# A decoder trunk on one core: the first norm made from the banks in which x is turned, and two weight splits moved in the attention

## The chip, the core and the metric

The kernel runs on one core of a Trainium2 chip. Five engines work side by side, each through its own list of instructions, and meet only at semaphores: TensorE (matrix products, called PE in the profile), VectorE (DVE), ScalarE (ACT), GpSimd (POOL) and SyncE (SP), which here only starts DMAs. The metric is the device time of one execution in microseconds, as a median over runs.

## The reference

Two layers over x of 256 tokens by 1024 columns, all in float32. Each layer adds half a SwiGLU feed-forward (2816 wide), a token mixer, and half a second feed-forward, each behind an RMS norm; a final norm ends it.

```
x = x + 0.5 * swiglu(rmsnorm(x, g1), w_gate, w_up, w_down)
h = rmsnorm(x, g_mix)
x = x + (hybrid_gdn_shortconv(h, ...) if layer == 0 else sliding_window_attention(h, ...))
x = x + 0.5 * swiglu(rmsnorm(x, g2), ...)

rmsnorm(x, g) = x * rsqrt(mean(x * x) + 1e-6) * g
swiglu(x)     = (silu(x @ w_gate) * (x @ w_up)) @ w_down
attention: 16 query heads, 4 key and value groups, window 128, rotary, a sink per head;
           p = exp(s - mx) / (sum(exp(s - mx)) + exp(sink - mx));  o = p @ v;  o @ w_o + b_o
```

## The kernel before

**Products.** Every float32 matrix is split in two parts that TensorE takes at full rate: a high part (a rounded copy) and a low part (the difference). A product is three matmuls: high by high (L349), low activation by high weight (L350), high activation by low weight (L354).

**Weights.** All weights stream through a ring of three slots in chunks of 1 MB (128 x 2048), numbered over the whole program. For each, SyncE loads `raw` (`load`, L302; it waits until the low half of the chunk three before is made), ScalarE makes `w_hi` (`split_hi`, L310; it waits until TensorE has used the chunk three before), VectorE makes `w_lo` (`split_lo`, L324; `split_lo_half`, L330, does it in two instructions). TensorE uses the chunk in `column_chunk` (L357, 48 matmuls of 256 columns), `down_chunk` (L624) or, in the attention, `token_chunk` (L1419) and `out` (L1544).

**Layout of x.** x is kept transposed in `xT`, as four pairs of 128-row tiles. At the start x is loaded in two column halves (L1807, L1808), TensorE turns it pair by pair into the four banks ACC (L1976), VectorE copies each bank to `xT` (L444), ScalarE makes the high half of h = x times the norm's weight (L419) and VectorE its low half (L431). The squares for the norm (L407), their sum (`norm_sum`, L459, VectorE, three additions), the sum over rows on TensorE (`norm_ss`, L392), the reciprocal (`norm_var`, L469) and the root (`norm_rstd`, L477) go beside the first matmuls, since the norm's factor is applied to the results of the projections. The first feed-forward takes chunk 0 (gate) and 1 (up), then `norm_ss`, chunk 2 (gate of the next group), chunk 3 (its up) and chunk 4 (the first down chunk); TensorE waits for `var_ready`, which the reciprocal raises, before chunk 3, since that chunk goes to the bank in which the sum stood. The first down chunk waits for `act_ready`, the low half of the gated activation (L582). ACC is free for the down products only when x is out of it.

**Order.** Each engine's order is written out by hand in the blocks at the end (L1801 to L1987). In the first stage ScalarE makes all high halves of h, the high half of chunk 0 in two pieces (L317), four squares, loads the table of the root, makes the high halves of chunks 1 and 2, starts the loads of the constants (`load_rest`, L1773: 832 KB and four small ones, on ScalarE's DMA queue), and goes on with chunks 3 and 4.

**Attention.** `swa_tensor` (L1415) takes six projection chunks c to c+5, and between and behind them, for four groups of heads, the scores (L1477), the turning of the probabilities (L1496), the values (L1510), the turning of the outputs (L1523) and the output projection, whose chunks 0 to 3 are c+6 to c+9. `soft` (L1684, VectorE) masks the scores and finds the maxima, `exps` (L1608, ScalarE) makes the exponentials; the turned probabilities of a group leave three banks, two by ScalarE (L1623) and one by VectorE (L1715), and the scores of the group two later wait for these copies. On VectorE the low half of chunk c+7 (output chunk 1) stands at the end of step m=4 and that of c+8 (output chunk 2) at the end of m=5, ahead of the copy of group 1.

## Time and profile before

| | us |
|---|---|
| median of 3 runs (lowest to highest) | 1023.87 (1023.36 to 1026.7) |
| the profiled execution's own time | 1026.56 |
| its span, first to last instruction | 1024.8 |
| TensorE busy (share of the span) | 996.1 (97%) |
| VectorE busy | 623.9 (61%) |
| ScalarE busy | 474.7 (46%) |
| GpSimd busy | 70.6 (7%) |
| mean granted TensorE clock | 0.995 |

Busy times are of one profiled execution; the span leaves out the short stretches around the first and the last instruction. A line of a timeline gives the start, the duration, the engine, the source line, what is written and read, how many of the same stand in the row, and in brackets how long the engine was idle before and what ended that idle time. Matmuls overlap, so the start of one is before the end of the last.

### The profile page before, as it was taken

Reading aid. Unit: us, or ns where it says so; the run is one execution under the profiler, and the core shown is the slowest. Engines: PE = TensorE matmul, PEld = TensorE weight load, DVE = VectorE, ACT = ScalarE, POOL = GpSimd, SP = SyncE. Lnnn points to the kernel's source line nnn. Section 1 sums busy time; section 2 is a strip of 40 time slices with the busy share of each in tenths; the row PEclk is TensorE's granted clock in tenths of the full one; section 3 lists DMA queues with packets and bytes.
Section 4 is the critical chain, followed back from the end, with each engine's and each line's share of the span. In section 5 each row is a group of like instructions: output and inputs, shape, how many; then the busy total and the mean of one; then the engine's idle time right before and its main releaser. Section 6 shows DMA issues by size and latency. Waiting matters only on the chain.

```text
span 1024.8 us, 19751 instructions
## 1 busy us (share of the span) xinstructions
PE 996.1 (97%) x8302; PEld 976.0 (95%) x8302; DVE 623.9 (61%) x651; ACT 474.7 (46%) x521; POOL 70.6 (7%) x63
## 2 busy tenths in 40 slices
PE   6999999999999999999999999999998999999997
PEld 6999999988999999999999999999997999999996
DVE  5755555788764376555548655555788376555553
ACT  5543444645553265443446543443656264443442
POOL 0110010100000001010110101010100001100100
PEclk9999999999999999999999999999999999999999
DMA  7666565454422246656665665656443045566651
GB/s 245 219 210 195 197 204 183 146 152 136 124 86 80 83 164 207 205 173 198 199 196 170 212 196 174 205 174 231 158 165 110 15 139 190 190 193 192 203 184 42
DMA packets 136035, 172.80 MB, mean 169 GB/s; under 512 B 4293, under 2 KB 123322, under 8 KB 135994
## 3 DMA queue, kind: packets, MB, share of 16 engines
q1 hardware_dynamic: 134176, 171.26, 51.7%
q10 hardware_dynamic: 1818, 0.96, 0.3%
q8 instruction: 31, 0.51, 0.2%
q14 instruction: 10, 0.08, 0.0%
HBM read 171.15 MB, written 1.05 MB: 168 GB/s over the span
## 4 chain that ended last, share of the span: by engine, by line
PE 87%; DVE 7%; ACT 3%; DMA 1%; issue 1%; POOL 0%; DVEq 0%; POOLq 0%; SPq 0%; ACTq 0%
PE bank L349 24%; PE bank L350 24%; PE bank L354 24%; PE bank L638 6%; DVE w_lo L327 2%; PE bank L1429 2%; ACT w_hi L315 1%; DMA raw<-in_ffn_w_up 1%; PE bank L873 1%; PE bank L857 1%; PE bank L868 1%; DMA work<-in_x 1%; DVE work L1272 1%; ACT h_hi_rest L419 0%; PE bank L1489 0%
## 5 line engine op out<-in xcount | busy, mean ns | idle before, releaser
L327 DVE TENSOR_TENSOR w_lo<-raw,w_hi 128x2048 fp32r<-128x2048 f32 x154 | 354.4, 2301 | 190.0 <-ACT w_hi L315 190.0
L349 PE MATMUL bank<-h_hi_rest,w_hi 128*128 128x256 f32 x1428 | 394.8, 278 | 0.4 <-DVE h_lo_rest L431 0.4
L350 PE MATMUL bank<-h_lo_rest,w_hi 128*128 128x256 f32 x1428 | 393.7, 277 | 0.0
L354 PE MATMUL bank<-h_hi_rest,w_lo 128*128 128x256 f32 x1428 | 385.2, 277 | 0.0
L315 ACT ACTIVATE w_hi<-raw 128x2048 fp32r<-128x2048 f32 x159 | 302.7, 1909 | 155.7 <-PE bank L354 139.7
L349 PEld LDWEIGHTS bank<-h_hi_rest,w_hi 128*128 128x128 f32 x1428 | 269.2, 188 | 0.8 <-DVE h_lo_rest L431 0.6
L350 PEld LDWEIGHTS bank<-h_lo_rest,w_hi 128*128 128x128 f32 x1428 | 269.1, 188 | 0.0
L354 PEld LDWEIGHTS bank<-h_hi_rest,w_lo 128*128 128x128 f32 x1428 | 264.1, 188 | 0.0
L349 PE MATMUL bank<-act_hi,w_hi 128*128 128x256 f32 x480 | 132.7, 276 | 1.1 <-DVE act_lo L582 1.1
L354 PE MATMUL bank<-act_hi,w_lo 128*128 128x256 f32 x480 | 132.6, 276 | 0.0
L350 PE MATMUL bank<-act_lo,w_hi 128*128 128x256 f32 x480 | 132.6, 276 | 0.0
L615 POOL TENSOR_TENSOR silu_r<-silu,work 128x512 f32<-128x512 f32 x44 | 60.5, 1375 | 785.9 <-ACT silu L528 785.9
L528 ACT ACTIVATE silu<-gate 128x512 f32<-128x512 f32 x44 | 27.8, 631 | 145.5 <-DVE gate L570 145.5
L349 PEld LDWEIGHTS bank<-act_hi,w_hi 128*128 128x128 f32 x480 | 90.1, 188 | 1.3 <-issue 1.3
L350 PEld LDWEIGHTS bank<-act_lo,w_hi 128*128 128x128 f32 x480 | 90.2, 188 | 0.0
L354 PEld LDWEIGHTS bank<-act_hi,w_lo 128*128 128x128 f32 x480 | 90.1, 188 | 0.0
L538 ACT ACTIVATE act_hi<-act 128x512 fp32r<-128x512 f32 x40 | 25.3, 633 | 132.0 <-PE bank L354 86.1
L349 PE MATMUL bank<-h_hi_first,w_hi 128*128 128x256 f32 x204 | 60.8, 299 | 7.0 <-DVE w_lo L341 3.5
L582 DVE TENSOR_TENSOR act_lo<-act,act_hi 128x512 fp32r<-128x512 f32 x40 | 27.7, 692 | 62.7 <-ACT act_hi L538 62.7
L354 PE MATMUL bank<-h_hi_first,w_lo 128*128 128x256 f32 x204 | 57.1, 280 | 0.0
L350 PE MATMUL bank<-h_lo_first,w_hi 128*128 128x256 f32 x204 | 56.4, 277 | 0.0
L349 PE MATMUL bank<-m_hi,w_hi 128*128 128x256 f32 (+1 forms) x200 | 55.8, 286 | 0.0
(276 smaller groups left out, 1258.1 us busy)
## 6 DMA issues: line engine op xcount, KB each, us to landing
raw<-in_ffn_w_up SPq DMA_DIRECT2D x44, 1024.0 KB, 5.3
raw<-in_ffn_w_down SPq DMA_DIRECT2D x44, 1024.0 KB, 4.8
raw<-in_ffn_w_gate SPq DMA_DIRECT2D x43, 1024.0 KB, 5.4
raw<-in_hyb_w_in SPq DMA_DIRECT2D x14, 1024.0 KB, 5.3
raw<-in_swa_w_qkv SPq DMA_DIRECT2D x6, 1024.0 KB, 5.0
raw<-in_hyb_w_out SPq DMA_DIRECT2D x4, 1024.0 KB, 5.6
raw<-in_swa_w_o SPq DMA_DIRECT2D x4, 1024.0 KB, 5.2
work<-in_x SPq DMA_DIRECT2D x2, 512.0 KB, 5.8
```

Source lines behind the costliest of these rows:

```text
L315: nc.scalar.activation(w_hi[slot(ch)][:], raw[:, slot(ch), :], ACT.Copy).then_inc(hi_split, 1)
L327: nc.vector.tensor_tensor(w_lo[slot(ch)][:], raw[:, slot(ch), :], w_hi[slot(ch)][:].bitcast(F32), ALU.subtract).then_inc(lo_split, 1)
L349: nc.tensor.matmul(out_ap, w_hi[s][:, wcols], mv_hi, start=start, stop=False, skip_group_check=True)
L350: i = nc.tensor.matmul(out_ap, w_hi[s][:, wcols], mv_lo, start=False, stop=False, skip_group_check=True)
L354: return nc.tensor.matmul(out_ap, w_lo[s][:, wcols], mv_hi, start=False, stop=stop, skip_group_check=True)
L528: nc.scalar.activation(silu[:], gate[:], ACT.Silu).then_inc(silu_ready, 1)
L538: nc.scalar.activation(hi.rearrange("p a b -> p (a b)"), act[:], ACT.Copy) \
L582: nc.vector.tensor_tensor(lo.rearrange("p a b -> p (a b)"), act[:], hi.rearrange("p a b -> p (a b)").bitcast(F32), ALU.subtract).then_inc( ...
L615: nc.gpsimd.tensor_tensor(silu_r[:].rearrange("p (a s) -> p a s", a=2), silu[:].rearrange("p (a s) -> p a s", a=2), over_rows(rstd_half[:] ...
L638: last = nc.tensor.matmul(o, st[:, k, tok], mv[s][:, cols], start=False, stop=False, skip_group_check=True)
L857: i = mm(head((AUX, AUX2)[b], h), one(step_m[n % 2], b, h), one(inv, b, h), start=True, stop=True)
L1429: i = mm(bk[:, b * CW:(b + 1) * CW], st[kt][:, b * P:(b + 1) * P], mv[s][:, kt * CW:(kt + 1) * CW], start=(start and n_pass == 0), stop=(s ...
```

## The change

x is loaded in three parts: two quarters of the columns on SyncE's queue and the half behind them on ScalarE's, between the loads of the norms' weights. In the first norm ScalarE and VectorE read x straight from the banks in which it was turned, and VectorE's four copies to `xT` are replaced by four of ScalarE (`keep_x`), one ahead of chunk 3's high half and three behind it. The high half of chunk 1 stands ahead of the squares, that of chunk 2 behind them and ahead of the table. The low half of chunk 0 is made in two pieces (`first_lo`) between the products of h, and TensorE takes the low products of a stage's first chunk in two halves of the rows. VectorE sums the squares ahead of chunk 2's low half, which is made in two pieces, and makes chunk 3's low half behind the reciprocal. In all four feed-forwards TensorE waits for `var_step` (the addition ahead of the reciprocal) in place of `var_ready`. The loads of the constants go to SyncE's queue, behind the first group's. TensorE multiplies a matrix of ones eight times ahead of the turning of x (`warm`). In the attention the low halves of output chunks 1 and 2 are moved on VectorE to ahead of and behind the last group's softmax.

```diff
+        def first_lo(dve, half):
+            dve.wait_ge((first_half_split, hi_split)[half], 1)
+            cols = slice(half * 1024, (half + 1) * 1024)
+            nc.vector.tensor_tensor(w_lo[0][:, cols], raw[:, 0, cols], w_hi[0][:, cols].bitcast(F32),
+                                    ALU.subtract).then_inc((first_lo_half, lo_split)[half], 1)
...
-              .then_inc((lo_half_split, lo_split)[part], 1)
+              .then_inc((half_done or lo_half_split, lo_split)[part], 1)
...
-                pe.wait_ge(lo_split, number(ch) + 1)
-                for ft in range(HG):
-                    for kt in range(KT):
-                        last = step(kt, ft, False, kt == KT - 1, 1)
+                for half in range(2):
+                    if first_chunk and half == 0:
+                        pe.wait_ge(first_lo_half, 1)
+                    else:
+                        pe.wait_ge(lo_split, number(ch) + 1)
+                    for ft in range(HG):
+                        for kt in range(half * KT // 2, (half + 1) * KT // 2):
+                            last = step(kt, ft, False, kt == KT - 1, 1)
             else:
                 for ft in range(HG):
                     if early is not None and ft == 0:
-                        pe.wait_ge(lo_half_split, early)
+                        pe.wait_ge(*early)
...
+        def turned(j):
+            return ACC[j][:]
+        def first_norm_scalar(act_e):
+            for j in range(PAIRS):
+                act_e.wait_ge(acc_done, j + 1)
+                for kt in (2 * j, 2 * j + 1):
+                    g = norm_column(0) + kt
+                    i = nc.scalar.activation(h_hi[kt], ACC[j][:, (kt % 2) * SEQ:(kt % 2 + 1) * SEQ], ACT.Copy,
+                                             scale=vecT[:, g:g + 1])
+                i.then_inc(h_hi_ready, 1)
+                if j % 2:
+                    first_split(act_e, j // 2)
+            split_hi(act_e, (1, 0), check=False)
+            for j in range(PAIRS):
+                act_e.wait_ge(h_ready, j + 1)
+                nc.scalar.activation(sq[:, j, :], turned(j), ACT.Square).then_inc(sq_ready, 1)
+            split_hi(act_e, (2, 0), check=False)
+            load_table(ACT.Sqrt)
+        def keep_x(act_e, j):
+            pair = xT[:, 2 * j:2 * j + 2, :].rearrange("p a b -> p (a b)")
+            nc.scalar.activation(pair, turned(j), ACT.Copy).then_inc(x_updated, 1)
+        def first_norm_vector(dve):
+            for j in range(PAIRS):
+                dve.wait_ge(h_hi_ready, j + 1)
+                for kt in (2 * j, 2 * j + 1):
+                    g = norm_column(0) + kt
+                    i = nc.vector.scalar_tensor_tensor(out=h_lo[kt],
+                                                       in0=ACC[j][:, (kt % 2) * SEQ:(kt % 2 + 1) * SEQ],
+                                                       scalar=vecT[:, g:g + 1], in1=h_hi[kt].bitcast(F32),
+                                                       op0=ALU.mult, op1=ALU.subtract)
+                i.then_inc(h_ready, 1)
+                if j % 2:
+                    first_lo(dve, j // 2)
...
                 if before_pair is not None:
                     before_pair(j)
                 act_e.wait_ge(x_updated, PAIRS * n + j + 1)
-                if n:
-                    act_e.wait_ge(sq_summed, n)
-                    act_e.wait_ge(ss_ready, n)
+                act_e.wait_ge(sq_summed, n)
+                act_e.wait_ge(ss_ready, n)
                 for kt in (2 * j, 2 * j + 1):
                     g = norm_column(n) + kt
                     i = nc.scalar.activation(h_hi[kt], xT[:, kt, :], ACT.Copy, scale=vecT[:, g:g + 1])
                 i.then_inc(h_hi_ready, 1)
-                if n:
-                    square(j)
...
-                if n == 0:
-                    nc.vector.tensor_copy(pair, banks[j][:]).then_inc(x_updated, 1)
-                elif bias is None:
+                if bias is None:
...
+        def load_rest(sp):
+            sp.dma_start(kon[:, P:K_END], t["constants"][:, P:K_END]).then_inc(rest_loaded, 16)
+            sp.dma_start(sinks[:], t["swa_sinks"][0].partition_broadcast(P)).then_inc(rest_loaded, 16)
...
+            sp.wait_ge(wba_cleared, 1)
+            sp.dma_start(wba_pad.rearrange("p (k c) -> p k c", k=KT)[:, :, 0:8],
+                            t["hyb_w_in"][0].rearrange("(k p) f -> p k f", p=P)[:, :, 4 * KEY:4 * KEY + 8]) \
...
             group(0)
+            if f == 0:
+                load_rest(sp)
             with sp.Fori(1, NG - 1) as i:
                 group(i)
...
-            column_chunk(pe, (c0 + 1, 0), UP, h_hi, h_lo, early=n + 1)
+            column_chunk(pe, (c0 + 1, 0), UP, h_hi, h_lo, early=(lo_half_split, n + 1))
...
-            column_chunk(pe, (c0 + 2, 0), AUX2, h_hi, h_lo)
-            pe.wait_ge(var_ready, n + 1)
+            column_chunk(pe, (c0 + 2, 0), AUX2, h_hi, h_lo, early=(first_lo_half, 2) if f == 0 else None)
+            pe.wait_ge(var_step, n + 1)
             column_chunk(pe, (c0 + 3, 0), AUX, h_hi, h_lo)
...
-                if m:
+                if m in (1, 2, 3):
                     split_lo(dve, (c + m + RING, 0))
             copy_probs(1)
             lo_o(0)
+            split_lo(dve, (c + 4 + RING, 0))
             soft(3)
+            split_lo(dve, (c + 5 + RING, 0))
             norm_o(1)
...
-            sp.dma_start(x_in[:, :, 0:D // 2], xt[:, :, 0:D // 2]).then_inc(x_loaded, 16)
-            sp.dma_start(x_in[:, :, D // 2:D], xt[:, :, D // 2:D]).then_inc(x_loaded2, 16)
+            sp.dma_start(x_in[:, :, 0:D // 4], xt[:, :, 0:D // 4]).then_inc(x_loaded, 16)
+            sp.dma_start(x_in[:, :, D // 4:D // 2], xt[:, :, D // 4:D // 2]).then_inc(x_loaded2, 16)
...
             for k, name in enumerate(("ffn1_norm", "mix_norm", "ffn2_norm")):
+                if k == 1:
+                    act_e.dma_start(x_in[:, :, D // 2:D], xt[:, :, D // 2:D]).then_inc(x_loaded3, 16)
...
-                    norm_scalar(act_e, n, lambda j: j >= 2 and first_split(act_e, j - 2))
-                    split_hi(act_e, (1, 0), check=False)
-                    split_hi(act_e, (2, 0), check=False)
-                    load_rest(act_e)
+                    first_norm_scalar(act_e)
+                    keep_x(act_e, 0)
                 else:
                     norm_scalar(act_e, n, (lambda j: j < 2 and split_hi(act_e, (c - 1 + j, 0))) if mixed else None)
                     if mixed:
                         split_hi(act_e, (c + 1, 0))
                     split_hi(act_e, (c + 2, 0))
                 split_hi(act_e, (c + 3, 0))
-                if kind == "swa":
+                for j in range(1, PAIRS if n == 0 else 1):
+                    keep_x(act_e, j)
+                if n == 0 or kind == "swa":
...
-                norm_vector(dve, n, banks, ready,
-                            vecT[:, V_BO:V_BO + KT] if n and stages[n - 1][0] == "swa" else None,
-                            (c - 1, 0) if mixed else None)
...
                 if n == 0:
-                    split_lo(dve, (c, 0))
+                    first_norm_vector(dve)
+                else:
+                    banks, ready = update(n)
+                    norm_vector(dve, n, banks, ready,
+                                vecT[:, V_BO:V_BO + KT] if stages[n - 1][0] == "swa" else None,
+                                (c - 1, 0) if mixed else None)
                 for part in range(2):
                     split_lo_half(dve, (c + 1, 0), part, kind == "swa")
                 if n == 0:
                     dve.wait_ge(vec_turned, 2)
                     nc.vector.tensor_copy(vecT[:, FIRST_VEC:NVEC], AUX2[:, FIRST_VEC:NVEC]).then_inc(vec_ready, 1)
-                if kind == "swa":
+                if n == 0:
+                    norm_sum(dve, n)
+                    for part in range(2):
+                        split_lo_half(dve, (c + 2, 0), part, half_done=first_lo_half)
+                elif kind == "swa":
                     norm_sum(dve, n)
...
                 norm_var(dve, n)
+                if n == 0:
+                    split_lo(dve, (c + 3, 0))
                 dve.wait_ge(rstd_ready, n + 1)
...
+            def warm(times):
+                for k in range(times):
+                    nc.tensor.matmul(AUX2[:, 0:P], ones[:], ones[:], start=True, stop=True)
+            pe.wait_ge(set_up, 1)
+            warm(4)
             pe.wait_ge(ident_loaded, 16)
             pe.wait_ge(first_vec_loaded, 16)
             nc.tensor.transpose(AUX[:, 0:FIRST_VEC], vec_rows[0:FIRST_VEC, :], ident[0:FIRST_VEC, 0:FIRST_VEC]) \
               .then_inc(vec_turned, 1)
-            pe.wait_ge(x_loaded, 16)
+            warm(4)
             for j in range(PAIRS):
-                if j == PAIRS // 2:
-                    pe.wait_ge(x_loaded2, 16)
+                if j <= PAIRS // 2:
+                    pe.wait_ge((x_loaded, x_loaded2, x_loaded3)[j], 16)
                 for kt in (2 * j, 2 * j + 1):
                     for b in range(TB):
                         o = (kt % 2) * SEQ + b * P
```

## Rows read from the trace of the kernel before

**Rows 1.** windows of the span: us, busy us of each engine (instructions), clock, DMA
```profile
0.00:41.00 41.00, 30.34 (x219) 28.86 (x220) 24.74 (x30) 21.95 (x29) 3.77 (x13) 1.00 0.80 255
41.00:320.00 279.00, 275.48 (x2400) 272.92 (x2400) 181.60 (x203) 133.53 (x140) 17.02 (x12) 1.00 0.50 159
```

**Rows 2.** timeline of TensorE, start stage: start us, us, line, operands [idle before <-releaser]
```profile
11.49 0.55 PE L349 MATMUL bank<-h_hi_first,w_hi 128*128 128x256 f32 x1 [1.25 <-ACT w_hi L321]
...
14.19 0.41 PE L349 MATMUL bank<-h_hi_rest,w_hi 128*128 128x256 f32 x1
...
20.50 0.38 PE L349 MATMUL bank<-h_hi_first,w_hi 128*128 128x256 f32 x1 [1.31 <-DVE w_lo L341]
...
25.99 0.28 PE L354 MATMUL bank<-h_hi_rest,w_lo 128*128 128x256 f32 x1
26.42 0.67 PE L397 MATMUL bank<-sq,mean_ones 128*128 128x256 f32 x2 [0.16 <-DVE sq L466]
...
33.17 0.38 PE L349 MATMUL bank<-h_hi_first,w_hi 128*128 128x256 f32 x1 [0.58 <-DVE var L475]
...
40.17 0.36 PE L349 MATMUL bank<-act_hi,w_hi 128*128 128x256 f32 x1 [1.08 <-DVE act_lo L582]
```

**Rows 3.** timeline of VectorE, start stage
```profile
7.79 1.47 DVE L444 COPY xT<-bank 128x512 f32<-128x512 f32 x2 [4.45 <-PE bank L1976]
...
19.22 2.36 DVE L341 TENSOR_TENSOR w_lo<-raw,w_hi 128x1024 fp32r<-128x1024 f32 x2 [2.32 <-ACT w_hi L315]
...
31.36 1.75 DVE L475 RECIPROCAL var<-var 128x256 f32<-128x256 f32 x1
```

**Rows 4.** timeline of ScalarE, start stage
```profile
10.20 1.04 ACT L321 ACTIVATE w_hi<-raw 128x1024 fp32r<-128x1024 f32 x1
...
13.69 2.18 ACT L407 ACTIVATE sq<-xT 128x512 f32<-128x512 f32 x4
15.88 1.28 ACT L294 ACT_TABLE_LOAD   x1
...
17.29 1.90 ACT L315 ACTIVATE w_hi<-raw 128x2048 fp32r<-128x2048 f32 x1
...
41.28 3.71 ACT L315 ACTIVATE w_hi<-raw 128x2048 fp32r<-128x2048 f32 x2
```

**Rows 5.** DMA issues at 1.18, 3.37 and 24.13 us: KB, us to landing
```profile
work<-in_x SPq DMA_DIRECT2D x1, 512.0 KB, 5.3
...
raw<-in_ffn_w_up SPq DMA_DIRECT2D x1, 1024.0 KB, 10.7
...
raw<-in_ffn_w_gate SPq DMA_DIRECT2D x1, 1024.0 KB, 9.3
```

**Rows 6.** timeline of TensorE, attention
```profile
759.54 1.97 PE L1489 MATMUL bank<-work 128*128 128x256 f32 x8 [0.78 <-ACT work L1606]
...
762.16 0.36 PE L1429 MATMUL bank<-w_hi,h_hi_first 128*128 128x256 f32 x1
...
791.20 3.78 PE L1489 MATMUL bank<-work 128*128 128x256 f32 x8 [3.77 <-DVE work L1715]
...
796.34 0.37 PE L349 MATMUL bank<-m_hi,w_hi 128*128 128x256 f32 x1
...
809.49 1.09 PE L1505 MATMUL bank<-kon,work 128*128 128x128 f32 x8
```

**Rows 7.** timeline of VectorE, attention
```profile
788.26 2.28 DVE L327 TENSOR_TENSOR w_lo<-raw,w_hi 128x2048 fp32r<-128x2048 f32 x1
```

**Rows 8.** timeline of ScalarE, attention
```profile
787.03 1.09 ACT L1623 ACTIVATE work<-bank 128x512 f32<-128x512 f32 x2 [1.70 <-PE bank L1507]
...
805.23 0.60 ACT L1628 ACTIVATE m_hi<-bank 128x512 fp32r<-128x512 f32 x1 [0.74 <-PE bank L1529]
```

**Rows 9.** windows of TensorE, attention: us, busy us (count), clock, DMA
```profile
787.20:791.20 4.00, 0.23 (x3) 0.79 0.00 0
791.20:792.00 0.80, 0.80 (x2) 0.50 0.56 47
```

More of the change, by code:

```diff
@@ L162, in trunk @@
         x_loaded2 = sem("x_loaded2")
+        x_loaded3 = sem("x_loaded3")
         first_vec_loaded = sem("first_vec_loaded")
@@ L172, in trunk @@
         first_half_split = sem("first_half_split")
+        first_lo_half = sem("first_lo_half")
         vec_turned = sem("vec_turned")
@@ L328, in split_lo, with split_lo_half @@
                                     ALU.subtract).then_inc(lo_split, 1)
-        def split_lo_half(dve, ch, part, by_rows=False):
+        def first_lo(dve, half):
[3 more added lines that the diff above has]
+                                    ALU.subtract).then_inc((first_lo_half, lo_split)[half], 1)
+        def split_lo_half(dve, ch, part, by_rows=False, half_done=None):
             dve.wait_ge(hi_split, number(ch) + 1)
@@ L420, in norm_scalar @@
                 i.then_inc(h_hi_ready, 1)
-                if n:
-                    square(j)
-            for j in range(PAIRS if n == 0 else 0):
                 square(j)
@@ L1172, in hyb_tensor @@
                              (h_ready, PAIRS * n) if m == 0 else None, between if m else None,
-                             n + 1 if m == 1 else None)
+                             (lo_half_split, n + 1) if m == 1 else None)
                 for x in HYB_PLAN.get((m, 1), []):
@@ L1771, in swa_vector @@
             lo_o(3)
-        def load_rest(act_e):
-            act_e.dma_start(kon[:, P:K_END], t["constants"][:, P:K_END]).then_inc(rest_loaded, 16)
-            act_e.dma_start(sinks[:], t["swa_sinks"][0].partition_broadcast(P)).then_inc(rest_loaded, 16)
-            act_e.dma_start(gate_par[:, 0, :], t["gdn_a_log"][0].partition_broadcast(P)) \
-              .then_inc(rest_loaded, 16)
-            act_e.dma_start(gate_par[:, 1, :], t["gdn_dt_bias"][0].partition_broadcast(P)) \
-              .then_inc(rest_loaded, 16)
-            act_e.wait_ge(wba_cleared, 1)
-            act_e.dma_start(wba_pad.rearrange("p (k c) -> p k c", k=KT)[:, :, 0:8],
-                            t["hyb_w_in"][0].rearrange("(k p) f -> p k f", p=P)[:, :, 4 * KEY:4 * KEY + 8]) \
-                 .then_inc(rest_loaded, 16)
         stages = [("ffn", 0), ("hyb", 0), ("ffn", 1), ("ffn", 2), ("swa", 0), ("ffn", 3)]
         def update(n):
-            if n == 0:
-                return ACC, [(acc_done, j + 1) for j in range(PAIRS)]
             kind, f = stages[n - 1]
@@ L1918, in _ @@
                 mixed = n > 0 and stages[n - 1][0] != "ffn"
-                banks, ready = update(n)
                 if n == 1:
                     dve.wait_ge(vec_ready, 2)
-                norm_vector(dve, n, banks, ready,
-                            vecT[:, V_BO:V_BO + KT] if n and stages[n - 1][0] == "swa" else None,
-                            (c - 1, 0) if mixed else None)
                 if n == 0:
-                    split_lo(dve, (c, 0))
+                    first_norm_vector(dve)
[4 more added lines that the diff above has]
+                                (c - 1, 0) if mixed else None)
                 for part in range(2):
```

6 lines of the change are left out of this document (added).

## The prediction

> **What bounds the kernel now.** I read the windows of the span first. From 41 to 320 us TensorE is busy 275.48 of 279.00 us, in the first 41 us only 30.34 of 41.00 [rows 1]; the stretches behind are like the former. So the matrix stream sets the time and only its idle places can be won. The waits of TensorE then name two places: the start, and one wait of 3.77 us in the attention. The timeline of each engine over these two places gives the steps below.
>
> At the start the first real matmul begins at 11.49, released by ScalarE's first high half. Chunk 1 starts at 20.50 after 1.31 us idle, the norm's sum at 26.42 after 0.16, chunk 3 at 33.17 after 0.58, the first down chunk at 40.17 after 1.08 [rows 2]. In a dense stream matmuls start 0.117 us apart (20.50 to 25.99, 47 steps), and each is drawn 0.28 long, so that an idle figure leaves out some 0.16 us of the last one's drain. The first matmuls start 0.225 apart (11.49 to 14.19, 12 steps) and last 0.41 [rows 2]: the lower of TensorE's two levels.
>
> Profiled execution: 1026.56 us, span 1024.8, so 1.8 around it. The median of the runs shown is 1023.87. I return to these 2.7 us below.
>
> **The change, the start.** (a) First matmul. Its chain before: x lands 5.3 us after its issue at 1.18, so at 6.5 [rows 5]; a pair of tiles is turned by 7.79, VectorE copies it (two copies in 1.47, 0.7 each) [rows 3], and only then ScalarE makes the high halves of h, four until 10.2, and half of the weight's in 1.04 [rows 4]. The copy leaves this chain: 0.7 us. What both engines read changes from SBUF to a bank; the nearest rows are ScalarE's copies out of banks, 1.09 us for two of 128x512 [rows 8], against 2.18 for four squares out of SBUF [rows 4], 0.55 each both, so I take no difference, bounds -0.1 and +0.1 us per instruction. New first matmul: about 10.8.
>
> The landing of the first quarter is not in the trace. It has half the bytes of the 512 KB transfer (5.3 us [rows 5]) but is now issued beside the 512 KB on ScalarE's queue. Bounds: 4.6 us, and 6.0 if the third load takes two turns for one; I take 5.3, the row. The Trainium skill (DMA: Bandwidth & Descriptors, Issuing engines are not separate DMA queues) says that transfers of all issuing engines run on the same 16 DMA engines and interleave, and that a second engine only saves issue time: by it the quarter lands with the former half, as taken; without it, 0.7 us sooner. ScalarE would gain little from the latter, since the weight's first half is the next arrival.
>
> (b) Chunk 1. Its high half runs at 17.29 for 1.90, because ScalarE first makes four squares (13.69, 2.18) and loads a table (15.88, 1.28) [rows 4]; its low halves follow at 19.22, 2.36 for the two [rows 3]. The change puts this high half right behind the first chunk's. ScalarE then runs: from 7.6, eight high halves of h at 0.42 and two of the weight at 1.0, free at 13.2; w_up lands at 3.37 + 10.7 = 14.1 [rows 5]; high half until 16.0, first low half 17.2. TensorE meanwhile starts 0.7 sooner and keeps its own work of the first chunk, so it comes to chunk 1 at 18.3, later than 17.2: the idle 1.31 + 0.16 goes whole. What is late next is TensorE itself. Chunk 1 starts 2.2 us sooner. The first chunk's low halves, in two pieces of 1.2 between VectorE's products, end at 14.8, before they are wanted at 16. Their loop in halves is the same 16 matmuls; for the first chunk of the other stages it only changes the order, 0.
>
> (c) Norm's sum and the waits behind. Squares end at 18.2, the sum (2.4 us on VectorE, now ahead of chunk 2's low half) at 21, chunk 1 ends at 23.9: no wait. Chunk 2's low halves 21.1 to 23.5, in time for 24.3. Chunk 3 waited for the reciprocal (1.75 [rows 3]) behind a low half; TensorE now waits for the addition before it, at 25.1: no wait. The copies of x (four at 0.6 on ScalarE) stand before the table's use, end at 25.7 and are hidden by the reciprocal, which ends at 26.8. Chunk 3's low half is put behind the reciprocal: until 29.1, wanted at 30. Then root, high half of the down chunk, table, silu, GpSimd (2.2), three short steps: act ready at about 35.6, while TensorE ends chunk 3 at 35.7. So the three idles 0.16 + 0.58 + 1.08 and their drains 0.5 go, 2.3 in all, if act is no more than 0.1 late. Start in sum: 0.7 + 1.5 + 2.3 = 4.5, less 0.1 for small waits: **4.4 us**. Bounds 3.0 (the quarter late by 0.7 and act late by 0.7) and 5.9 (the clock rises before the first chunk: 15 steps at 0.1 less).
>
> The eight added matmuls of ones lie in TensorE's idle time before x lands; four take 0.9, the second four end at 4.1, before 6.5: 0. Without that cover each costs 0.23.
>
> (d) The constants' loads go from ScalarE's queue to SP's, behind the loads of chunks 3 and 4 and ahead of chunk 5's. Chunk 3's is no longer disturbed. Chunk 5 landed 9.3 us after 24.13 [rows 5]; it would now be issued at 23.5 and stand behind 832 KB more, some 2.4 us (from x at 6.5 to w_up at 14.1 land 2.5 MB, 3.0 us for one): 35.2. ScalarE took it at 41.28 [rows 4] and will want it at 36.8. Slack 1.6: 0; if it is gone, each us late costs one.
>
> (e) TensorE's wait for the addition in the three later feed-forward stages: none had an idle there, 0.
>
> **The attention.** Before: ScalarE copies the turned probabilities of group 1 from 787.03 [rows 8]; VectorE's third copy should follow at 788.1 but out chunk 2's low half (788.26, 2.28) stands ahead [rows 7], and the scores of group 3, which need that bank, start only at 791.20 [rows 6]. Then they run slowly: from 791.20 to 796.34, against 2.62 for the same 16 at 759.54 to 762.16 [rows 6]. The granted clock says why: 0.79 in the idle stretch, 0.50 from 791.20 [rows 9], the lower level. That is 5.14 - 2.62 = 2.5 us.
>
> After: chunk 1's low half is also gone from before the last projection's evacuation, which moves from 780.4 to 779.1 (TensorE ends that chunk then), so turned scores of group 1 start at 784.7 without their 0.8 of waiting, ScalarE copies from 786.2, VectorE at 787.3, scores(3) at 788.0: 3.2 sooner. TensorE is idle 1.5 us instead of 3.77, which I take to be too short for the clock to fall; so the 16 end at 790.7, 5.7 sooner. The two low halves now stand later on VectorE: m_lo of group 0 until 788.9, chunk 1's until 791.1 (wanted at 792.1), softmax of group 3 until 795.4, chunk 2's until 797.7, wanted at 797.4: a new wait of 0.3. Then the exponentials: before, from the start of the high half of o at 805.23 to the next turning at 809.49 is 4.26 [rows 6, 8]; the high half now comes at 799.9, so that turning is at 804.2, which gives **5.3 us** (2.8 without the clock's part). Behind it all is as before; the loads of the next stage, held by these low halves, come 10 and 7 us later and are wanted 27 us after that.
>
> **Sum:** 4.4 + 5.3 = 9.7 us; 1026.56 - 9.7 = 1016.9. Against the median: 1026.56 less 2.5 is 1024.1, close to 1023.87, so I read the median as runs in which the clock did not fall. There the change is worth 4.4 + 2.8 = 7.2: 1016.7. Both ways 1016.9 or so; that is -0.7%.
>
> **Rivals.**
> 1. *The attention's wait is only handed on.* If the two low halves behind the softmax reach group 3's softmax or chunk 2's wait more than I reckon (the chain on VectorE has under 1 us of play, 791.1 against 792.1), some 2.5 us of idle return: 1019.4. For it: three VectorE steps now stand in a row there. Against: ScalarE's exponentials, not the softmax, end last.
> 2. *The start is bound by arrivals.* If the third load beside the first two delays x and both weight halves by 1 us, and act is late by 1 us, the start gives 2.4: 1018.9. For it: three loads in flight at once. Against: the bytes ahead of w_up are the same.
> 3. *Slower: the low level lasts.* The changed start has a pause between transposes and matmuls and, if high halves are late, one inside the first chunk. Should the clock stay at 1.2 GHz, each step costs 0.225 - 0.117 = 0.108 more; over the first four chunks' 192 steps beyond the 15 slow now, 19 us: 1036. The gain is used up from 7.2 / 0.108 = 67 further slow steps. Against: before, the level rose although there was a pause of 1.3 us.
> 4. *It doesn't do what it says:* the copy by VectorE in the attention waits for ScalarE after all and the start is held by w_up; under 3 us: 1022.
>
> **How the numbers follow.** Forecast 0.72, its own range 1015.2 to 1018.6 (4.4 within 3.0 to 5.9); rival 1 0.09, rival 2 0.10, rival 4 0.05, rival 3 0.04. The range reaches over rivals 1 and 2: 1015.0 to 1019.8. A change within 0.3% (3.1 us) is about what cannot be told from none. Faster by more: forecast, rivals 1 and 2, 0.91; within: rival 4, 0.05; slower: 0.04.
>
> **What will show it.** VectorE's copy off the chain and the first matmul at 10.8; chunk 1's first matmul at 18.3 with no idle; no idle ahead of the norm's sum and of chunk 3; the first down chunk near 35.8 where 40.17 stood; scores(3) after 1.5 us of idle with the clock at 1.0 throughout; the turning at 809.49 about 9.7 sooner. The forecast is wrong if the first down chunk is after 37.5, if a pause of 3 us is left in the attention, or if chunk 5 makes TensorE wait.

## The result, and the profile after

| | before | after |
|---|---|---|
| median of 4 runs (lowest to highest), us | 1024.67 (1023.36 to 1026.7) | 1015.41 (1014.45 to 1016.08) |
| profiled execution's own time, us | 1026.56 | 1014.88 |
| its span, us | 1024.8 | 1013.1 |
| mean granted TensorE clock | 0.995 | 0.999 |

The ratio of the run times is 0.9896, 95% interval 0.9881 to 0.991: faster by 1.0%. The two medians in the table are 9.3 us apart (0.991, the upper end of that interval), the two profiled executions 11.7 us. The head of the profile's page of after, with the busy time and share of each engine:

```profile
span 1013.1 us, 19786 instructions
...
PE 996.4 (98%) x8318; PEld 976.6 (96%) x8318; DVE 621.3 (61%) x649; ACT 476.7 (47%) x525; POOL 70.3 (7%) x63
```

TensorE's busy time is what it was; its idle time is shorter. The timeline of TensorE over the start, in the columns of [rows 2], which it answers:

```profile
1.00 2.07 PE L2024 MATMUL bank<-ones 128*128 128x128 f32 x8 [1.00 <-POOL neg_half L1871]
...
5.96 3.82 PE L2039 MATMUL bank<-kon,work 128*128 128x128 f32 x16 [0.67 <-DMA work<-in_x]
10.18 0.54 PE L358 MATMUL bank<-h_hi_first,w_hi 128*128 128x256 f32 x1 [0.40 <-ACT w_hi L323]
...
16.35 0.39 PE L358 MATMUL bank<-h_hi_first,w_hi 128*128 128x256 f32 x1
...
22.05 0.59 PE L410 MATMUL bank<-sq,mean_ones 128*128 128x256 f32 x2
...
33.52 0.36 PE L358 MATMUL bank<-act_hi,w_hi 128*128 128x256 f32 x1
```

The lines from 16.35 on bear no bracket: the four waits of 1.31, 0.16, 0.58 and 1.08 are gone. The first down chunk starts 6.65 us sooner. The first chunk takes 6.17 us (10.18 to 16.35); it took some 7.5 before. That is a matter of TensorE's two levels. Here at the start the level can only be read from the spacing of the products: the granted clock of before reads 1.00 from 11.5 to 14.5 us, where they start 0.215 apart. A later row of the order-alone run below shows the same 0.215 under a granted clock of 0.50, so I call it the lower level here too.

ScalarE and VectorE over the same stretch, for [rows 4] and [rows 3]. ScalarE first:

```profile
7.18 0.48 ACT L426 ACTIVATE h_hi_first<-bank,vecT 128x256 fp32r<-128x256 f32 x1 [2.99 <-PE bank L2039]
...
8.84 1.06 ACT L323 ACTIVATE w_hi<-raw 128x1024 fp32r<-128x1024 f32 x1
...
13.12 1.92 ACT L317 ACTIVATE w_hi<-raw 128x2048 fp32r<-128x2048 f32 x1 [0.81 <-DMA raw<-in_ffn_w_up]
14.94 2.04 ACT L434 ACTIVATE sq<-bank 128x512 f32<-128x512 f32 x4
```

```profile
15.07 2.36 DVE L350 TENSOR_TENSOR w_lo<-raw,w_hi 128x1024 fp32r<-128x1024 f32 x2 [1.22 <-ACT w_hi L317]
```

Chunk 1's high half waits for its load and starts at 13.12 where 17.29 stood; its first low half (15.07 plus 1.2) is there at 16.3, when TensorE comes. Four squares out of a bank take 2.04 beside 2.18 out of SBUF. The transfers issued between 1 and 4 us (size, us from issue to landing), for [rows 5]:

```profile
raw<-in_ffn_w_gate SPq DMA_DIRECT2D x2, 512.0 KB, 6.9
raw<-in_ffn_w_up SPq DMA_DIRECT2D x1, 1024.0 KB, 9.9
...
work<-in_x ACTq DMA_DIRECT2D x1, 512.0 KB, 4.9
```

w_up, issued at 3.23, lands at 13.1 (issued at 3.37 and landed at 14.1 before), although as many bytes are ahead of it.

The attention, TensorE, for [rows 6]:

```profile
779.66 0.60 PE L1590 MATMUL bank<-kon,work 128*128 128x128 f32 x4
781.85 2.00 PE L1550 MATMUL bank<-work 128*128 128x256 f32 x8 [1.59 <-DVE work L1776]
783.68 1.05 PE L1554 MATMUL bank<-work 128*128 128x128 f32 x8
...
797.79 1.09 PE L1566 MATMUL bank<-kon,work 128*128 128x128 f32 x8
```

and the granted clock there (columns as in [rows 9]):

```profile
778.00:781.00 3.00, 2.26 (x21) 1.00 0.00 0
781.00:784.00 3.00, 2.15 (x11) 1.00 0.00 0
```

The pause is 1.59 instead of 3.77, the clock stays up, and the 16 products of the scores take 2.6 us instead of 5.1. The turning that stood at 809.49 is 11.70 sooner. Of the 6.65 of the start 6.2 are left when the attention's edits begin (the scores of group 2 stand at 772.66 instead of 778.85; 0.3 is lost between 57 and 205 us, for a reason not looked for), so the attention gives 5.5. Nothing is given back behind it. TensorE's three longest remaining waits (total us, times, longest):

```profile
PE bank L358 <- DVE w_lo L350: 2.2, 2, 1.1
PE bank L358 <- DVE w_lo L329: 1.6, 1, 1.6
PE bank L1550 <- DVE work L1776: 1.6, 1, 1.6
```

### The profile page after: what moved, and what is told of

It is laid out like the page before. It is cut to its first block, busy times and chain, and to the rows that moved or that the text cites. A ratio compares the mean times of both kernels' runs of the same rounds, so it can differ in the third digit from the quotient of the medians.

```text
span 1013.1 us, 19786 instructions
## 1 busy us (share of the span) xinstructions
PE 996.4 (98%) x8318; PEld 976.6 (96%) x8318; DVE 621.3 (61%) x649; ACT 476.7 (47%) x525; POOL 70.3 (7%) x63
## 4 chain that ended last, share of the span: by engine, by line
PE 91%; DVE 5%; ACT 2%; issue 1%; DMA 0%; DVEq 0%; POOLq 0%; POOL 0%; SPq 0%; ACTq 0%
PE bank L358 25%; PE bank L359 25%; PE bank L363 25%; PE bank L699 6%; PE bank L1490 2%; DVE w_lo L329 1%; ACT w_hi L317 1%; PE bank L934 1%; PE bank L918 1%; PE bank L929 1%; DVE work L1333 1%; DMA work<-in_x 0%; PE bank L1550 0%; PE bank L1581 0%; PE bank L1580 0%
## 5 line engine op out<-in xcount | busy, mean ns | idle before, releaser
L329 DVE TENSOR_TENSOR w_lo<-raw,w_hi 128x2048 fp32r<-128x2048 f32 x152 | 349.8, 2301 | 187.7 <-ACT w_hi L317 187.7
```

Of the source, the lines that this page charges most:

```text
L329: nc.vector.tensor_tensor(w_lo[slot(ch)][:], raw[:, slot(ch), :], w_hi[slot(ch)][:].bitcast(F32), ALU.subtract).then_inc(lo_split, 1)
```

## The experiments

The theory after the result: both places work as forecast, but the start gets 2.3 us more than its 4.4. It has two causes: the first chunk's products run at the higher level of TensorE's clock, and the loads land up to 1 us sooner through the second queue. Rivals: the ones hold the clock up; the second queue adds nothing; the order of the work is all. A ratio below is against runs of the kernel before beside it on the same chip; in these four groups its median was 1025.93, 1027.03, 1026.97 and 1026.33 (9 to 21 runs each). Where a gain is given in us from a ratio, it is the ratio times that median.

**The changed kernel again.**

> The changed kernel again, as the yardstick of this call. Theory A (two gains at the start that the prediction set at nothing: TensorE's level is up from the first products because of the matmuls of ones, and every load lands about 1 us sooner because a second queue fills the slow first microseconds): ratio to the kernel before 0.988 to 0.991, the first down chunk at 33.5 us, where 40.17 stood. Rival B (the prediction's sum of 9.7 us holds and the rest is the scatter of the few runs of before): ratio 0.9905 to 0.993.

1015.33 us, 0.9901 (0.9885 to 0.9918); the first down chunk at 33.76. The result repeats.

**Without the ones.**

```diff
-            warm(4)
...
-            warm(4)
```

> The changed kernel without the eight matmuls of ones. Theory A: first product at 10.2 us as before, but the first products again 0.21 apart until about 14 us, so that the first chunk ends 1.3 to 2 us later, the first down chunk comes at 35 to 35.5 us instead of 33.5, and the kernel is 1.5 to 2 us slower than the changed one. Rival B (the ones do nothing, as predicted): 0.12 apart from the start all the same, the down chunk at 33.5, no difference in time.

1015.25 us, 0.9899 (0.9884 to 0.9914). TensorE's first products:

```profile
10.48 0.55 PE L358 MATMUL bank<-h_hi_first,w_hi 128*128 128x256 f32 x1 [0.40 <-ACT w_hi L323]
...
11.26 0.28 PE L359 MATMUL bank<-h_lo_first,w_hi 128*128 128x256 f32 x1
11.38 0.28 PE L358 MATMUL bank<-h_hi_rest,w_hi 128*128 128x256 f32 x1
```

From the fourth product on they last 0.28 and start 0.12 apart; the down chunk comes at 33.70. The ones are worth nothing that five runs tell, and they are not what holds the clock up. That rival falls.

**The attention alone.**

```diff
-                if m:
+                if m in (1, 2, 3):
...
+            split_lo(dve, (c + 4 + RING, 0))
             soft(3)
+            split_lo(dve, (c + 5 + RING, 0))
```

> The kernel before with only the attention's part of the change (the two low halves moved on VectorE). Theory A and the prediction: the pause before the scores of group 3 shrinks from 3.8 to 1.6 us, the clock stays up, 5.0 to 5.3 us less than a run of before in which the clock fell and 2.8 less than one in which it did not; as a median 3 to 4.5 us less than before, and a smaller spread of the runs. Rival C (the clock does not fall in the runs of before as a rule and the pause is only handed on): less than 1.5 us.

1020.99 us, 0.9954 (0.994 to 0.9967): 4.7 us by the ratio, not 2.8. The one wait left in the attention above 1 us:

```profile
789.41 1.99 PE L1489 MATMUL bank<-work 128*128 128x256 f32 x8 [1.59 <-DVE work L1715]
```

**The start alone** (the changed kernel with the edit above undone).

> The changed kernel with the attention's two low halves back in their old places. If start and attention are independent: start worth 6 to 6.5 us (40.17 to 33.6 in the profiles), so 5.5 to 7 us less than before, and with the attention alone (4.9 us) the two add up to the whole 10.4. The clock falls again in the pause of the attention in most runs. Rival: the two overlap, and the start alone gives 8 or more.

1020.89 us, 0.9935 (0.9921 to 0.9949): 6.7 us by the ratio, 6.1 between the medians; the down chunk at 33.50. The old pause is back, and the clock behind it falls again:

```profile
786.70 3.78 PE L1550 MATMUL bank<-work 128*128 128x256 f32 x8 [3.76 <-DVE work L1776]
```

```profile
783.00:786.70 3.70, 0.00 (x0) 0.79 0.00 0
786.70:789.00 2.30, 2.30 (x6) 0.50 0.66 186
```

The two parts make 11.4 together by the ratios, against 10.2 to 10.7 for the whole and 11.7 in the profiles: they add up within the intervals. In the profiles the gain over the attention is 5.5 in the one part alone and 0.0 in the other.

**The pause of before, filled.** Twelve products of ones into an unused bank ahead of the scores of group 3; the wait for the last projection's evacuation stands ahead of them.

```diff
             turn_o(0)
-            scores(3)
             pe.wait_ge(swa_evacuated, SWA_IN)
+            for k in range(12):
+                mm(GATE[:, 0:P], ones[:], ones[:], start=True, stop=True)
+            scores(3)
```

> The kernel before with twelve products of ones (written to a bank that is free) in the 4 us pause of the attention ahead of the scores of group 3; nothing else is changed. Theory A (the pause lets the clock fall, in most runs of before): the granted clock stays at 1.00 through the pause, the 16 products of that group take 2.6 us instead of 5.1, the kernel is 1.5 to 2.5 us faster than before. Rival C (the clock falls for another reason or only in the profiled run): 0 to 0.5 us.

1025.2 us, 0.9984 (0.9975 to 0.9993).

```profile
787.21 2.84 PE L1568 MATMUL bank<-ones 128*128 128x128 f32 x24
791.14 1.99 PE L1489 MATMUL bank<-work 128*128 128x256 f32 x8 [1.09 <-DVE work L1717]
792.97 1.05 PE L1493 MATMUL bank<-work 128*128 128x128 f32 x8
```

The scores start where they did (791.14 beside 791.20) and end 2.5 sooner. The ratio gives 1.6 us (1.8 between the medians). So the clock's fall is a cost of its own. That most runs of before have it is not seen directly, as one run of each kernel is profiled, but the mean granted clock of every run fits: it is 0.996 or less in 34 of the 56 runs of before beside these experiments, and in none of the 17 with the pause filled or shortened (11 here, 6 of the attention alone).

**x on one queue** (the changed kernel).

```diff
             sp.dma_start(x_in[:, :, D // 4:D // 2], ...).then_inc(x_loaded2, 16)
+            sp.dma_start(x_in[:, :, D // 2:D], ...).then_inc(x_loaded3, 16)
...
-                if k == 1:
-                    act_e.dma_start(x_in[:, :, D // 2:D], ...).then_inc(x_loaded3, 16)
```

> The changed kernel with the last half of x loaded on SyncE's queue too, behind the two quarters and ahead of the weights. Theory A: the first quarter lands as early or earlier (5.5 to 5.9 us), but the half of x and all weights land up to 1 us later (the first weight half at 9.5 instead of 8.6, w_up at 14.1 instead of 13.1), so chunk 1 starts 0.5 to 1 us later: 0.5 to 1 us slower than the changed kernel. Rival D (the second queue does nothing to the sum of the traffic, the loads land as before): no difference.

1018.02 us, 0.9921 (0.9905 to 0.9937); 2.7 later than the run beside it. The timeline of TensorE:

```profile
8.37 1.09 PE L2038 MATMUL bank<-kon,work 128*128 128x128 f32 x8 [1.52 <-DMA work<-in_x]
11.21 0.55 PE L358 MATMUL bank<-h_hi_first,w_hi 128*128 128x256 f32 x1 [1.75 <-ACT w_hi L323]
...
19.33 0.36 PE L358 MATMUL bank<-h_hi_first,w_hi 128*128 128x256 f32 x1
```

The stretch from 3.0 to 4.5 us (last columns: DMA share, GB/s), first of before, then of after, then of this kernel:

```profile
3.00:4.50 1.50, 0.17 (x1) 1.00 0.94 179
```

```profile
3.00:4.50 1.50, 0.17 (x1) 1.00 0.98 325
```

```profile
3.00:4.50 1.50, 0.17 (x1) 1.00 0.93 209
```

With all of x on one queue the same 16 DMA engines are as busy and move a third less. The first quarter lands sooner (4.5 instead of 5.9), the rest later: the weight's first half at 9.9 (8.6), w_up at 14.3 (13.1). Part of that is the time of issuing: with one load more ahead of them on the queue both are issued 0.5 later. The remaining 0.8 and 0.7 are slower transfer. TensorE starts 1.0 later, and here its first chunk runs slowly (8.1 us; the granted clock reads 0.50 from 10.5 us on), so that the down chunk is at 36.57.

**The same, with six small loads of the norms' and mixers' vectors behind w_up.** They are issued beside x.

```diff
-            act_e.dma_start(...)     # six loads, 0.5 to 24 KB each
...
             load(sp, (c0 + 1, 0), wu[:, :, 0:CW], check=c0 >= RING)
+            sp.dma_start(...)        # the same six
```

> The kernel of the single queue (x in three loads, all on SyncE's queue) with the six small loads moved behind w_up on SyncE's queue, so that ScalarE's queue holds only the first norm's weights. If it was the small loads beside x that made the first microseconds slow (rival E), the rate from 3 to 4.5 us goes to 300 GB/s or more, the first weight half lands at 8.6 to 9.0 us and the time comes to within 1 us of the changed kernel. If it is the single queue (theory A), the rate stays near 210 GB/s, the weight half lands near 9.9, and the time stays 2 to 3 us above the changed kernel.

1018.22 us, 0.9914 (0.9898 to 0.9929). The weight's half lands at 9.9 still, and 3.0 to 4.5 us moves 220 GB/s: the single queue is slow, not the small loads. In this profile the clock stayed up in spite of pauses of 1.49 and 2.06. It is not the typical run: it took 1015.87 with a mean clock of 0.999, the other three 1018.22 to 1018.36 with 0.994 to 0.996.

```profile
8.07 1.09 PE L2042 MATMUL bank<-kon,work 128*128 128x128 f32 x8 [1.49 <-DMA work<-in_x]
11.22 0.36 PE L358 MATMUL bank<-h_hi_first,w_hi 128*128 128x256 f32 x1 [2.06 <-ACT w_hi L323]
...
34.95 0.36 PE L358 MATMUL bank<-act_hi,w_hi 128*128 128x256 f32 x1
```

**One queue, both pauses filled with ones** (`warm(3)` ahead of the third pair's turning and behind the last).

> The kernel of the single queue with three products of ones in each of the two pauses of TensorE at the start (between the second and third pair of x, and ahead of the first product of the weights). That kernel lost 2.7 us against the changed one: by theory A about 1 us through later loads and the rest because TensorE's clock fell over the two pauses (0.50 from 10.5 to 13.5 us). With the pauses filled the clock should be 1.00 throughout, the first chunk should take 6.1 instead of 8.1 us, and 1.3 to 2 us come back. If arrivals alone decide, nothing comes back.

1016.14 us, 0.9895 (0.988 to 0.991); the first product at 11.44 with the clock up, the down chunk at 35.14. Against 36.57 the clock's share of that kernel's loss is 1.4 us; the 1.6 left against 33.52 is the later start. The ratio shows none of that 1.6. The intervals are 1.5 us to either side, so this stays open.

**The second queue alone** (the kernel before, second half of x issued by ScalarE between the norms' loads).

> The kernel before with only the second half of x loaded on ScalarE's queue, behind the first small load and ahead of the other small ones. Theory A (a second queue with large packets fills the slow first microseconds): 300 GB/s or more from 3 to 4.5 us where before had 179; w_up lands at 13.1 instead of 14.1 us; but ScalarE's squares and table still stand ahead of chunk 1's high half, so the time falls by 0.5 to 1 us only. Rival D (only the issue times on SyncE's queue matter): w_up lands at 13.6, since its issue is 0.5 us earlier, with the rate from 3 to 4.5 us as before.

1027.23 us, 1.0007 (0.9997 to 1.0017). 281 GB/s from 3.0 to 4.5, w_up at 12.9, 1.2 sooner than before (0.7 of it by its earlier issue at 2.71), and yet:

```profile
20.55 0.39 PE L349 MATMUL bank<-h_hi_first,w_hi 128*128 128x256 f32 x1 [1.28 <-DVE w_lo L341]
...
41.24 0.35 PE L349 MATMUL bank<-act_hi,w_hi 128*128 128x256 f32 x1 [1.24 <-DVE act_lo L582]
```

In the old order the squares and the table stand ahead of chunk 1's high half, so an earlier load waits. The down chunk is even 1.1 later than before: the constants are issued 1.0 sooner (15.88), and the load of chunk 3 lands at 27.8 instead of 26.7, so that chunk 3 waits 1.60 instead of 0.58.

**The clock alone** (the kernel before, three products of ones between the turning of x and the first product).

> The kernel before with three products of ones in TensorE's pause between the turning of x and the first product. If the pause is what keeps the first products slow, they should be 0.12 apart from the start or soon after and the first chunk ends 1 to 1.5 us sooner; but chunk 1 waits for its low half, which ScalarE's squares and table hold until 20.5 us whatever TensorE does, so no time is won: ratio 0.999 to 1.001. Rival: the faster first chunk is worth its 1.3 us in this order too, ratio 0.9985 or less.

1025.46 us, 0.9998 (0.9988 to 1.0007).

```profile
11.60 0.36 PE L349 MATMUL bank<-h_hi_first,w_hi 128*128 128x256 f32 x1 [0.78 <-ACT w_hi L321]
...
17.06 0.39 PE L354 MATMUL bank<-h_hi_first,w_lo 128*128 128x256 f32 x1 [0.99 <-DVE w_lo L327]
...
20.61 0.39 PE L349 MATMUL bank<-h_hi_first,w_hi 128*128 128x256 f32 x1 [1.31 <-DVE w_lo L341]
```

The first chunk's products run at the higher level and wait for their weights instead. Neither part of the surplus is worth anything in the old order.

**The order alone** (the changed kernel without ones, x in two halves on SyncE's queue as before).

> The changed kernel with x loaded as in the kernel before (two halves on SyncE's queue) and without the ones, so that the new order of the engines' work is tried on the old arrivals. If the prediction's arithmetic of the start was right for the arrivals that it assumed and what it missed is the second queue and the clock: first product near 10.8 us, the first down chunk at 35.3 to 36.0, start worth 4.4 us, the kernel 1.5 to 2.5 us slower than the changed one (ratio to before 0.9915 to 0.993). Rival: the arithmetic itself was too low, the down chunk comes at 33.5 to 34.5 on the old arrivals too, ratio 0.989 to 0.991.

1017.73 us, 0.9915 (0.9901 to 0.9928).

```profile
10.58 0.35 PE L358 MATMUL bank<-h_hi_first,w_hi 128*128 128x256 f32 x1 [0.65 <-ACT w_hi L323]
...
17.02 0.39 PE L358 MATMUL bank<-h_hi_first,w_hi 128*128 128x256 f32 x1 [0.17 <-DVE w_lo L350]
...
34.08 0.36 PE L358 MATMUL bank<-act_hi,w_hi 128*128 128x256 f32 x1
```

The higher level comes with the new order; the pause ahead of it is 0.65 instead of 1.25. The loads (w_up at 13.8) now come 0.2 late for chunk 1. By the ratio it is 1.4 to 1.9 us above the whole change (0.0014 and 0.0019, with intervals that overlap); at the down chunk the profile says 0.6. What the second queue and the quarter add to the order lies between these; its exact size stays open.

The profiled execution itself is 2.5 us above that of after, and the start accounts for only 0.7 of it (up to 308 us). Behind that, at 310 us, the clock falls once:

```profile
308.74 1.84 PE L970 MATMUL bank<-o_par,sq 128*128 128x1 f32 x16
...
311.18 0.41 PE L358 MATMUL bank<-h_hi_rest,w_hi 128*128 128x256 f32 x1
311.40 0.41 PE L359 MATMUL bank<-h_lo_rest,w_hi 128*128 128x256 f32 x1
```

```profile
310.45:313.70 3.25, 3.25 (x17) 0.51 0.03 7
```

TensorE has no idle time there. Ahead of the fall stand 16 products of one column. From them to the next group of this kind it is 17.0 us where after has 15.4, so the fall costs 1.6. The same stands in the profiles of the attention alone and of the start alone, and in none of the other thirteen. The three kernels share no edit that the others lack, so no edit explains it. What sets it off was not tried; it may be part of the scatter of the run times.

**Waiting for the reciprocal again.**

```diff
-            pe.wait_ge(var_step, n + 1)
+            pe.wait_ge(var_ready, n + 1)
```

> The changed kernel with TensorE waiting for the reciprocal again ahead of chunk 3 in all four feed-forwards. Prediction: the reciprocal ends at 24.9 us in the first stage and chunk 3 starts at 28.0 (VectorE now makes it ahead of chunk 3's low half), so the shorter wait is worth nothing at all: same time as the changed kernel, 1015.3, within 0.5 us. Rival: it was worth the 0.74 us of idle that stood there, 1016.

1015.58 us, 0.9896 (0.9881 to 0.9912), down chunk at 33.48: the shorter wait is worth nothing, once the reciprocal stands ahead of the low half.

**The constants on ScalarE's queue again.**

```diff
-            if f == 0:
-                load_rest(sp)
...
                     first_norm_scalar(act_e)
+                    load_rest(act_e)
                     keep_x(act_e, 0)
```

> The changed kernel with the loads of the constants on ScalarE's queue again, behind the table of the root. Prediction: chunks 3 and 4 land later (before 9.8 and 9.2 us after their issue, now 5.3 and 5.7), chunk 3 issued at 13.9 would land at 22 to 23.5; its high half is wanted at 20.7, and its low half ends at 27.0 against 28.0 wanted: so 0 to 1 us slower than the changed kernel. Rival: the queue of the constants makes no difference, below 0.3 us.

1017.59 us, 0.9907 (0.9894 to 0.9921).

```profile
26.89 1.92 ACT L317 ACTIVATE w_hi<-raw 128x2048 fp32r<-128x2048 f32 x1 [1.52 <-DMA raw<-in_ffn_w_down]
```

```profile
34.62 0.36 PE L358 MATMUL bank<-act_hi,w_hi 128*128 128x256 f32 x1 [0.98 <-DVE act_lo L641]
```

Here a wait of about 1 us for the gated activation stands where there was none. It comes by chunk 4, not by chunk 3 as I expected: chunk 3 lands 5.5 us after its issue, as in after, but chunk 4 takes 9.3 instead of 5.7, and the table and `silu` stand behind its high half on ScalarE. In time the cost is 1.1 us by the ratio, with intervals that overlap.

**A version beyond both.** Two waits of 1.1 for `w_lo` are left at chunk 1 of the two later feed-forwards behind a mixer, since the root's table is loaded ahead of that chunk's high half.

```diff
-            load_table(ACT.Sqrt)
+            if before_pair is None:
+                load_table(ACT.Sqrt)
...
                         split_hi(act_e, (c + 1, 0))
+                        load_table(ACT.Sqrt)
```

> The changed kernel and one edit more: in the two feed-forwards behind the hybrid mixer and the attention ScalarE loads the table of the root behind the high half of the second chunk instead of ahead of it, as the change did in the first stage. TensorE waits 1.1 us there for the low half of that chunk, twice. The table takes 1.3 us. Expected: both waits go, 2.0 to 2.2 us faster than the changed kernel, 1013.2. Rival: the wait goes to the next chunk or to the norm's sum, less than 1 us.

1013.32 us (1012.99 to 1014.12), 0.987 (0.9854 to 0.9885). The first line of TensorE's waits is gone. What it has in its place:

```profile
PE bank L410 <- DVE sq L513: 0.9, 1, 0.9
```

So at the first of the two places most of the wait is handed on to the norm's sum (0.9 of 1.1), as the rival said; at the second it is gone. The median is 2.3 us below the kernel that waits for the reciprocal (1015.58), which ran beside it and is as fast as the changed one; the intervals just overlap. The profiled execution is 1.8 below that of after. It is the fastest of all.

## Why the prediction came out as it did

The mechanism held at both places. What failed are the sizes of two terms: the start, forecast as 4.4 us and measured as 6.65 at the first down chunk, and the conversion of the profile's sum to the median, which made 7.2 of 9.7 where the ratios give 10.2 to 10.7.

**Right.** The first matmul no longer waits for VectorE's copy, and operands in a bank cost as much as in SBUF. Chunk 1, the norm's sum, chunk 3 and the first down chunk have no idle; from chunk 1 to the down chunk 17.17 us were measured and 17.5 forecast. The attention: 5.5 against 5.3, scores(3) after 1.59 of idle where 1.5 was forecast, the clock at 1.0. The wait at out chunk 2 is too small to be drawn. The ones cost nothing, though their own price was wrong: four take 2.07 us, not 0.9. The edit of the three later stages' wait is worth 0. Chunk 5 lands at 31.1, not 35.2, and nobody waits. Rivals 1 to 4 are all out: no wait was handed on, arrivals did not bind, the level did not last low, and no part failed to do what it says.

**Step (a), "I take 5.3, the row", and w_up at 14.1.** The quarter lands 4.7 after its issue, near my lower bound, and the weight's half at 8.6 instead of 9.6, so the first product is at 10.18, not 10.8: 0.6. I held that as many bytes ahead mean the same landing. From issue to landing w_up takes 9.9 to 10.3 us in the eight profiles with x on two queues and 10.5 to 10.9 in the eight with x on one. The Trainium skill (DMA: Bandwidth & Descriptors, Issuing engines are not separate DMA queues) has a second issuing engine save issue time only. Issue time is part of it here, 0.5 to 0.7 of the 1.2 in two of the pairs above, but only 0.14 of the 0.9 between before and after. For the rest the measurement decides against that rule in the first microseconds: 179 or 209 GB/s on one queue, 325 on two.

**Step (b), "keeps its own work of the first chunk".** I kept the low level for it, 7.5 us; it took 6.17: 1.3. The bound of 5.9 had this case (15 steps at 0.1) but I gave it no part of the forecast. Before, the turning ran at the low level and was followed by 1.25 us of idle; in the profile of after it ran there too (16 in 3.82), but 0.40 of idle was left, and the level rose. The step that takes the copy off the chain shortens the pause that I had left out of the clock's sum. That the shorter pause is the cause is shown for the old order (filled with ones there, the first chunk runs high) and argued for the new. It is not the pause alone: in the repetition the turning was already fast, and the level held over 1.37. All told the first chunk ran high in ten of eleven profiles of the new order and low in all four of the old one that nothing filled; what makes the one exception is open. It pays only because the high half of chunk 1 starts at 13.12; with w_up at 14.1 and a low half at 17.2 a chunk that ended at 16.35 would have waited 0.9. Both errors, 0.6 and 1.3, and 0.3 behind chunk 1 make the 2.25.

Of that surplus 0.45 is lost again ahead of the attention, and 0.2 is won there: 11.7 in place of 9.7.

**Step (d)** was 0, and for chunk 5 it is. Moving the constants back costs some 1 us. Where the loads of chunks 3 and 4 would have met the constants I counted nothing, though the sentence on the undisturbed chunk 3 came near it; the one that counts is chunk 4.

**The conversion to the median** is the other error. I read 1023.87 as runs in which the clock did not fall, and took the attention as 2.8 there. Alone it is worth 4.7, and filling the pause 1.6. The 56 later runs of before show where the reading failed. Three of them have a mean granted clock of 1.0, and they took 1023.06 to 1023.81; the other 53 have 0.993 to 0.998 and took 1025.02 to 1029.01. So 1023.87 does look like a run without a fall. But such runs are few, and the medians of the four groups are 1025.9 to 1027.0: it was luck that two of the three runs shown were of this kind. On the sum of 9.7 against the profiled execution alone, 10.2 to 10.7 by the ratio is near; on 7.2 against the median it is not. A mean clock does not say where it fell: in the attention, at 310 us or elsewhere.

## What to carry to other kernels

Judge an early load together with the order of the work that takes it: alone it was worth 0 here, and under the new order between 0.6 (profile) and 2.7 us (medians, the clock's part in it). Where a pause is followed by steps of the slow kind, price the pause twice, once as idle time and once as the steps behind it, and ask of each edit whether it also removes the second. Before three runs are read as a state of the chip, compare their scatter with the effect claimed: 3.3 us from lowest to highest bears no statement on 2.5. Look at the granted clock of each run beside its time, and over the whole span of the profile, not only at the place of the edit.

## What the chip showed unexpectedly

- Two issuing queues in the first microseconds move more than one with the same bytes: 281 to 339 GB/s from 3.0 to 4.5 us in the eight profiles with two, 179 to 220 in the eight with one, at a DMA share of 0.76 to 0.99 throughout. What in the single queue costs it was not tried.
- The level of TensorE's clock behind a pause at the start, read from the spacing of the products, isn't a matter of the pause's length alone. It was low behind 1.25 (before, the attention alone, the filled attention pause, the second queue alone) and behind 1.52 and 1.75 (x on one queue), and high behind 1.36 to 1.46 (the repetition, the reciprocal, the constants) and 1.49 and 2.06 (small loads later).
- The clock can fall without any pause: to 0.50 for some 3 us at 310 to 319 us, behind 16 products of one column, in three of sixteen profiles of kernels that do the same work there, at a cost of 1.6 us. What decides it is open.
- In the attention, the pause of 3.8 us was followed by a lower level in all four profiles that have it unfilled (first eight products of the scores in 3.78, 3.78, 2.68 and 3.55 us), the one of 1.59 in none of eleven (1.99 or 2.00).
- A float32 product of 128 columns of ones is drawn as two rows, eight rows in 2.07 us at the very start, and 24 in 2.84 in the attention: 0.26 and 0.12 for each.
